# First modulation of a two-block transformer kernel: a third weight quarter split into two passes, quarters loaded in halves, two pieces given to GpSimd

## The reference, cut to what matters

```python
act_lat, act_ctx = jax.nn.silu(c), jax.nn.silu(c_ctx)          # two vectors of 1024

def ada_params(cond_act, w, b):
    mod = cond_act @ w + b                                     # w: 1024 x 3072
    return jnp.split(mod, 3, axis=-1)                          # shift, scale, gate
...
sh_l, sc_l, gt_l = ada_params(act_lat, w_ada[i], b_ada[i])
u_lat = rms_norm(h_lat, norm_g[i]) * (1.0 + sc_l[:, None, :]) + sh_l[:, None, :]
sh_c, sc_c, gt_c = ada_params(act_ctx, w_ada[i], b_ada[i])
...
p_lat = u_lat @ w_in                                           # the first big product
```

## Time and profile before

| what | value |
|---|---|
| median of 3 runs | 1294.01 us (1292.58 to 1297.1) |
| the profiled execution's own time | 1294.15 us |
| its span | 1292.4 us |
| PE busy | 1279.1 us, 99% of the span |
| DVE, ACT, POOL busy | 816.0, 656.4, 443.2 us |
| first matmul of the layer's first product | 42.85 us after the span's start |

### The profile page before, as it was taken

One profiled execution on the slowest core, in us unless ns is written; L12 is line 12 of the kernel. 1 busy time (PEld: TensorE's weight loads), 2 busy tenths in 40 slices (PEclk: granted clock), 3 DMA queues, 4 the chain that ended last, 5 costly groups with the idle time before them and its releaser, 6 DMA issues.

```text
span 1292.4 us, 17472 instructions
## 1 busy us (share of the span) xinstructions
PE 1279.1 (99%) x6553; PEld 1067.3 (83%) x6553; DVE 816.0 (63%) x1215; ACT 656.4 (51%) x1074; POOL 443.2 (34%) x203
## 2 busy tenths in 40 slices
PE   8999999999999999999999999999999999999998
PEld 4688788889988888877789889888888888888886
DVE  1795788865945457788657425406448768667676
ACT  4553777844523354766654544633355534455341
POOL 0234011137432394422234333344563322332310
PEclk9999999999999999999999999999999999999999
DMA  9972000066332153312133232233255243332301
GB/s 347 310 248 74 11 23 24 27 225 203 98 98 65 35 163 98 98 49 61 48 88 99 82 82 69 79 98 98 83 161 159 86 122 107 98 113 84 114 1 66
DMA packets 181401, 135.43 MB, mean 105 GB/s; under 512 B 10154, under 2 KB 154651, under 8 KB 181324
## 3 DMA queue, kind: packets, MB, share of 16 engines
q1 hardware_dynamic: 181122, 134.34, 34.3%
q10 hardware_dynamic: 202, 0.06, 0.0%
HBM read 129.66 MB, written 4.72 MB: 104 GB/s over the span
## 4 chain that ended last, share of the span: by engine, by line
PE 87%; DVE 4%; ACT 3%; DMA 2%; issue 2%; POOL 2%; SPq 0%; DVEq 0%; POOLq 0%; ACTq 0%
PE psum L2344 26%; PE psum L2346 26%; PE psum L2345 26%; PE psum L2556 2%; POOL w_lo L773 1%; DMA ada_w<-in_w_ada 1%; PE psum L2402 1%; PE psum L2546 1%; DVE out_rows L2277 1%; PE psum L2547 1%; PE psum L2820 1%; PE psum L2808 1%; ACT w_hi L881 1%; PE psum L2831 0%; DMA w_raw<-in_mla_w_out 0%
## 5 line engine op out<-in xcount | busy, mean ns | idle before, releaser
L773 POOL TENSOR_TENSOR w_lo<-w_raw,w_hi 128x1024 fp32r<-128x1024 f32 x148 | 381.6, 2584 | 658.3 <-ACT w_hi L881 623.2
L2344 PE MATMUL psum<-u_hi,w_hi 128*128 128x512 f32 (+1 forms) x704 | 267.1, 379 | 0.7 <-POOL w_lo L773 0.5
L2345 PE MATMUL psum<-u_lo,w_hi 128*128 128x512 f32 (+1 forms) x704 | 260.9, 371 | 0.0
L2346 PE MATMUL psum<-u_hi,w_lo 128*128 128x512 f32 (+1 forms) x704 | 260.8, 370 | 0.0
L881 ACT ACTIVATE w_hi<-w_raw 128x1024 fp32r<-128x1024 f32 x148 | 155.5, 1055 | 77.3 <-PE psum L2346 28.3
L2344 PE MATMUL psum<-y_hi,w_hi 128*128 128x512 f32 x416 | 162.2, 390 | 0.0
L2345 PE MATMUL psum<-y_lo,w_hi 128*128 128x512 f32 x416 | 161.9, 389 | 0.0
L2346 PE MATMUL psum<-y_hi,w_lo 128*128 128x512 f32 x416 | 161.9, 389 | 0.0
L2344 PEld LDWEIGHTS psum<-u_hi,w_hi 128*128 128x128 f32 x704 | 132.7, 189 | 26.7 <-issue 2.4
L2346 PEld LDWEIGHTS psum<-u_hi,w_lo 128*128 128x128 f32 x704 | 132.7, 188 | 23.3
L2345 PEld LDWEIGHTS psum<-u_lo,w_hi 128*128 128x128 f32 x704 | 132.9, 189 | 20.6 <-issue 0.2
(11 more groups left out here) (498 smaller groups left out, 2586.8 us busy)
## 6 DMA issues: line engine op xcount, KB each, us to landing
w_raw<-in_w_in SPq DMA_DIRECT2D x52, 512.0 KB, 3.8
w_raw<-in_w_up SPq DMA_DIRECT2D x32, 512.0 KB, 4.1
down_set<-in_w_down SPq DMA_DIRECT2D x32, 512.0 KB, 4.9
ada_back<-in_w_ada SPq DMA_DIRECT2D x7, 2048.0 KB, 10.8
w_raw<-in_fno_w_in SPq DMA_DIRECT2D x16, 512.0 KB, 4.0
ada_w<-in_w_ada SPq DMA_DIRECT2D x3, 2048.0 KB, 15.5
w_raw<-in_mla_w_in SPq DMA_DIRECT2D x11, 512.0 KB, 5.2
w_raw<-in_mla_w_out SPq DMA_DIRECT2D x8, 512.0 KB, 3.8
```

The lines of the kernel that those rows point to most:

```text
L773: pool.tensor_tensor(WL[:, j, :], RAW[:, j % 2, :], f(WH[:, j, :]), ALU.subtract).then_inc(lo_done, 1)
L2344: pe.matmul(out, ah, bh, start=first, stop=False, skip_group_check=more)
L2345: pe.matmul(out, ah, bl, start=False, stop=False, skip_group_check=more)
L2346: return pe.matmul(out, al, bh, start=False, stop=last, skip_group_check=more)
```

## The change

Quarter 2 is now treated as quarter 1 is: ACT makes its `QHI` (one buffer for both quarters, so quarter 1's pieces wait until quarter 2's have been used), and PE multiplies it in two passes. Quarters 2, 1 and 3 are loaded in two DMAs of 1 MB each, and quarter 3's halves are put behind weight tiles 0 and 1. Of each split quarter the first `QLOW` piece is made by POOL, the other three by DVE. On DVE the pieces of quarter 2 come ahead of `DIAG`, and the last two of quarter 1 behind `first_modulation(0)`. On ACT `split_hi` of weight tile 0 comes straight after the last `QHI` piece. Semaphore names and counts follow (not shown here). The core of the diff:

```diff
@@ sync
-            sp.dma_start(AQ[2][:], ada_weights(2)).then_inc(s_adaq[2], 16)
-            for q in (1, 3):
-                sp.dma_start(AQ[q][:], ada_weights(q)).then_inc(s_adaq[q], 16)
+            def ada_half(q, n):
+                sp.dma_start(AQ[q][:, 4 * n:4 * n + 4, :], ada_weights(q)[:, 4 * n:4 * n + 4, :]).then_inc(second_half[q] if n else s_adaq[q], 16)
+            for q in (2, 1):
+                ada_half(q, 0)
+                ada_half(q, 1)
...
-            load_tile(A0, None, 0, d["mla_w_in"][:, 0:P], KC)
-            load_tile(A0, None, 1, d["mla_w_in"][:, P:2 * P], KC)
+            for n in range(2):
+                load_tile(A0, None, n, d["mla_w_in"][:, n * P:(n + 1) * P], KC)
+                ada_half(3, n)
@@ gpsimd
+            for n, q in enumerate((2, 1)):
+                pool.wait_ge(x_copied, KC + 4 * n + 1)
+                pool.tensor_tensor(QLOW[q][:, 0:2, :], AQ[q][:, 0:2, :], f(QHI[:, 0:2, :]), ALU.subtract).then_inc(l_up, 1)
             for j in range(4):
                 split_lo(A0, None, j)
@@ scalar
+            def quarter_hi(q, n):
+                if n % 2 == 0:
+                    act.wait_ge(second_half[q] if n else s_adaq[q], 16)
+                if q == 1:
+                    act.wait_ge(diag_done, n) if n else act.wait_ge(l_up, 1)
+                act.activation(QHI[:, 2 * n:2 * n + 2, :], AQ[q][:, 2 * n:2 * n + 2, :], ACT.Copy).then_inc(x_copied, 1)
             ada_row_copy(0, 0, 1)
+            for n in range(4):
+                quarter_hi(2, n)
+            act.wait_ge(spread_mm, 2)
+            quarter_hi(1, 0)
+            quarter_hi(1, 1)
             ada_row_copy(1, 2, 2)
-            act.wait_ge(s_adaq[1], 16)
-            for n in range(4):
-                act.activation(QHI[:, 2 * n:2 * n + 2, :], AQ[1][:, 2 * n:2 * n + 2, :], ACT.Copy).then_inc(x_copied, 1)
+            quarter_hi(1, 2)
+            quarter_hi(1, 3)
+            split_hi(A0, None, 0)
...
-            ada_row_copy(2, 1, 4)
-            split_hi(A0, None, 0)
             for c in range(4):
+                if c == 2:
+                    ada_row_copy(2, 1, 4)
                 lat_hi(c)
@@ vector
             v.wait_ge(s_const, 16)
+            link(v.tensor_tensor(SEL4[:], IDENT[0:4, 0:2], IDENT[0:4, 2:4], ALU.add))
+            def quarter_lo(q, n):
+                v.wait_ge(x_copied, KC + (5 if q == 1 else 1) + n)
+                k = slice(2 * n, 2 * n + 2)
+                v.tensor_tensor(QLOW[q][:, k, :], AQ[q][:, k, :], f(QHI[:, k, :]), ALU.subtract).then_inc(diag_done, 1)
+            for n in range(1, 4):
+                quarter_lo(2, n)
             for m in range(TT):
                 v.tensor_scalar(DIAG[:, m, :], IDENT[:], RSC[:, m:m + 1], None, ALU.mult).then_inc(diag_done, 1)
-            link(v.tensor_tensor(SEL4[:], IDENT[0:4, 0:2], IDENT[0:4, 2:4], ALU.add))
             v.wait_ge(spread_mm, 1)
             v.tensor_copy(BROW[:], PB[:, 0:TOEP]).then_inc(bias_row, 1)
-            for n in range(4):
-                v.wait_ge(x_copied, KC + n + 1)
-                k = slice(2 * n, 2 * n + 2)
-                v.tensor_tensor(QLOW[:, k, :], AQ[1][:, k, :], f(QHI[:, k, :]), ALU.subtract).then_inc(diag_done, 1)
+            quarter_lo(1, 1)
...
                 first_modulation(half)
+                if half == 0:
+                    quarter_lo(1, 2)
+                    quarter_lo(1, 3)
@@ tensor
-            ada(2)
-            pe.wait_ge(diag_done, TT)
+            pe.wait_ge(cact_done, 4)
+            for k in range(KC):
+                pe.wait_ge(x_copied, KC + k // 2 + 1)
+                mm = pe.matmul(ada_row_bank(2)[0:4, :], CSPLIT[:, k, :], QHI[:, k, :], start=k == 0, stop=False)
+            mm.then_inc(spread_mm, 1)
+            for k in range(KC):
+                pe.wait_ge(diag_done, k // 2) if k >= 2 else pe.wait_ge(l_up, 1)
+                mm = pe.matmul(ada_row_bank(2)[0:2, :], CSPLIT[:, k, 0:2], QLOW[2][:, k, :], start=False, stop=k == KC - 1)
+            mm.then_inc(ada_mm, 1)
+            pe.wait_ge(diag_done, 3 + TT)
             for m in range(TT):
                 mm = pe.matmul(bank(3, P, m * P), ONES[:], DIAG[:, m, :], start=True, stop=True)
             mm.then_inc(spread_mm, 1)
             turn_row(0, 0)
             turn_row(1, 2).then_inc(ada_mm, 1)
```

More of the change, by code:

```diff
@@ L191, in build @@
         DIAG = at("rstd_diag", 160, [P, TT, P])
-        AROW = [at(f"ada_row{n}", 164 - 2 * n, [2, T]) for n in range(2)]
+        AROW = [at("ada_row0", 164, [2, T]), at("ada_row1", 162, [4, T])]
         AROW += [at("ada_row2", 166, [4, T]), at("ada_row3", 204, [2, T])]
@@ L200, in build @@
         AACC = [at("ada_sum0", 156, [P, T]), at("ada_sum1", 158, [P, T]), at("ada_sum2", 204, [P, T])]
-        QHI, QLOW = at("ada_second_hi", 120, [P, KC, T], f32r), at("ada_second_lo", 136, [P, KC, T], f32r)
+        QHI = at("ada_quarter_hi", 120, [P, KC, T], f32r)
+        QLOW = {2: at("ada_third_lo", 32, [P, KC, T], f32r), 1: at("ada_second_lo", 136, [P, KC, T], f32r)}
         CSPLIT, SEL4 = at("c_act_split", 155.875, [P, KC, 4], f32r), at("row_pairs", 154.625, [4, 2])
@@ L359, in build @@
         bias_row = sem("bias_row_done_then_down_lo_by_vector")
-        bias_out = sem("bias_stored")
+        bias_out = sem("ada_third_second_half_loaded_then_bias_stored")
         link_s = sem("vector_steps")
@@ L429, in build @@
         d_full = [[s_x[0], s_x[1], s_first, s_ctx], [s_bias, s_const, s_t5, s_dft]]
-        FULL0 = [[16, 16, 16, 16], [16, 16, 48, 80]]
+        FULL0 = [[16, 16, 16, 16], [32, 16, 48, 80]]
         d_sum, SUMS0 = cols_t, 1
@@ L505, in build @@
         ADA0 = 6
+        second_half = {2: bias_out, 1: s_bias, 3: kv_raw[0]}
+        UP0 = 2
         def ada_row_bank(q):
@@ L689, in _ @@
             sp.wait_ge(f_lo, KC)
-            sp.wait_ge(bias_out, 16)
+            sp.wait_ge(bias_out, 32)
             sp.dma_start(BIAS[:], bass.AP(toep, P - 1, [[TOEP - 1, P], [P * TOEP, MH], [1, T]])).then_inc(s_bias, 16)
@@ L921, in ada_row_copy @@
                 act.wait_ge(ada_mm, done)
-                act.activation(AROW[n][:], ada_row_bank(q)[0:4 if q == 1 else 2, :], ACT.Copy).then_inc(ada_row, 1)
-            ada_row_copy(0, 0, 1)
+                act.activation(AROW[n][:], ada_row_bank(q)[0:4 if q in QLOW else 2, :], ACT.Copy).then_inc(ada_row, 1)
+            def quarter_hi(q, n):
[4 more added lines that the diff above has]
+                act.activation(QHI[:, 2 * n:2 * n + 2, :], AQ[q][:, 2 * n:2 * n + 2, :], ACT.Copy).then_inc(x_copied, 1)
+            ada_row_copy(0, 0, 1)
+            for n in range(4):
[3 more added lines that the diff above has]
+            quarter_hi(1, 1)
             ada_row_copy(1, 2, 2)
-            act.wait_ge(s_adaq[1], 16)
-            for n in range(4):
-                act.activation(QHI[:, 2 * n:2 * n + 2, :], AQ[1][:, 2 * n:2 * n + 2, :], ACT.Copy).then_inc(x_copied, 1)
+            quarter_hi(1, 2)
+            quarter_hi(1, 3)
+            split_hi(A0, None, 0)
             def lat_hi(c):
@@ L981, in head_hi @@
             def head_hi(h):
-                act.wait_ge(kv_raw[h % 2], 16 * (h // 2 + 2) if h % 2 else 32 * (h // 2 + 1))
+                act.wait_ge(kv_raw[h % 2], 16 * (h // 2 + 2) if h % 2 else 16 + 32 * (h // 2 + 1))
                 act.wait_ge(raw_full[h % 2], raw_count(HD, None, h))
@@ L2071, in _ @@
             for h in range(GH):
[L2072 removed]
+                v.wait_ge(l_up, UP0 + h + 1)
                 v.tensor_scalar(MN[:, h, :], bank(h), COLS[:, gb + h:gb + h + 1], 0.0, ALU.add, ALU.min).then_inc(l_min, 1)
@@ L2399, in ada @@
                 for k in range(k0, k1):
-                    if q == 0 and k == 4:
-                        pe.wait_ge(s_first, 16)
+                    if k == 4:
+                        pe.wait_ge(s_first if q == 0 else second_half[q], 16)
                     mm = pe.matmul(ada_row_bank(q)[0:2, :], CACT[:, k, :], AQ[q][:, k, :], start=k == 0, stop=k == KC - 1)
@@ L2428, in _ @@
             turn_row(1, 2).then_inc(ada_mm, 1)
-            pe.wait_ge(cact_done, 4)
             for k in range(KC):
-                pe.wait_ge(x_copied, KC + k // 2 + 1)
+                pe.wait_ge(x_copied, KC + 4 + k // 2 + 1)
                 pe.matmul(ada_row_bank(1)[0:4, :], CSPLIT[:, k, :], QHI[:, k, :], start=k == 0, stop=False)
             for k in range(KC):
-                pe.wait_ge(diag_done, TT + k // 2 + 1)
-                mm = pe.matmul(ada_row_bank(1)[0:2, :], CSPLIT[:, k, 0:2], QLOW[:, k, :], start=False, stop=k == KC - 1)
+                pe.wait_ge(diag_done, 3 + TT + k // 2) if k >= 2 else pe.wait_ge(l_up, 2)
+                mm = pe.matmul(ada_row_bank(1)[0:2, :], CSPLIT[:, k, 0:2], QLOW[1][:, k, :], start=False, stop=k == KC - 1)
             mm.then_inc(ada_mm, 1)
```

10 lines of the change are left out of this document (5 added, 5 removed).

## The result

| kernel | median of its runs, us | runs | ratio to before, 95% interval |
|---|---|---|---|
| before | 1292.57 (1291.99 to 1297.10) | 14 | |
| changed | 1298.91 (1296.92 to 1300.58) | 14 | 1.0043 [1.0035, 1.0050] |

The ratio compares the means of the runs (1298.73 and 1293.13); the medians lie 6.3 us apart. The forecast was 1295.7 with a range of 1292.0 to 1298.0 and 9% for "slower": the time lies above the range. The profiled execution of the changed kernel took 1299.54 us, span 1297.8, against 1294.15 and 1292.4: 5.4 us more. Its page, busy time by engine, answers to the earlier trace rows: PE is still busy 99% of the span, and has 1.3 us more to do though its list is hardly longer.

A forecast was written before the change was run, and what follows sets the result against it. PE's list was taken to bound the kernel; with POOL and DVE excluding each other, quarter 3 would start at 37.49 instead of 35.96, so 1294.15 + 1.5 = 1295.7 us, range 1292.0 to 1298.0.

The forecast's parts named there:

- the reading: First 45 us: PE's list bounds the kernel, so the change counts by when the first big product can begin.
- the prices: First 45 us: durations of added work, such as hi pieces 0.95 apart, POOL's piece 2.34, SEL4's turn 1.05 us.
- The free sum: Start of quarter 3 without POOL and DVE waits: about 33.4 us, 2.5 us earlier, total 1291.6; chance 8%.
- the exclusion: POOL and DVE subtractions in the split quarters stop each other for a whole instruction; each new overlap is a wait.
- signs that I had named against the exclusion: DVE instructions at the overlaps lasting 1.22 and 0.16 us would make the prediction wrong by up to 4 us.
- the order at DIAG's boundary: DVE, after quarter 2's lo pieces, keeps its turn through DIAG to 28.46 us; POOL's quarter 1 piece waits.
- rival 1: POOL gets in between DVE's pieces and DIAG at 27.67; quarter 3 at 38.08, loss 2.1, 1296.3 us; chance 22%.
- the granted clock stayed 1.00: PE from 32 to 34 us before, busy 1.36 of 2 us at 2.4 GHz; so the clock was expected to hold.
- rival 4: PE's clock falls to 1.2 GHz for half of quarter 3, adding 3.5 us, to 1299.2 us; chance 5%.
- the base: Quarter 2 landing at 21.94; the profiled execution's 1294.15 us, also taken for the median of three, 1294.01.
- the halves, costed at nothing: Loads of quarters 2, 1, 3 in halves: no bytes moved, landings before they are needed, cost nothing.
- the rest of the list moves with the first product: After the first product, nothing else is late; later work shifts by the same amount.

The follow-up runs named there:

- e9_tile0_last_hi_filled: `e6_tile0_last` plus dummy PE matmuls only ahead of and within quarter 2's hi pass; 1292.86 us, ratio 0.9993.
- e5_filled_throughout: Changed kernel plus dummy PE matmuls in every gap from 20.9 us to the spread; 1295.63 us, ratio 1.0016.
- e2_pe_filled: Changed kernel plus eight dummy PE matmuls between quarter 2's lo pass and the wait for DIAG; 1298.86 us, ratio 1.0030.
- e4_loads_only: Kernel before with only the change's loads (halves, quarter 3 behind the first weight tiles), nothing split anew; 1293.02 us, ratio 0.9992.
- e7_tile0_last_filled: `e6_tile0_last` plus dummy PE matmuls in quarter 2's hi and lo passes, none ahead of DIAG; 1293.87 us, ratio 1.0004.
- e8_shift_only: Kernel before, nothing split and no load changed, plus 17 dummy PE matmuls ahead of quarter 3; 1298.26 us, ratio 1.0034.
- e10_loads_again: The kernel of `e4_loads_only` measured once more, against the kernel before; 1292.53 us, ratio 0.9987.
- e1_diag_first: Changed kernel with DIAG ahead of quarter 2's lo pieces on DVE, POOL keeping its two pieces; 1296.23 us, ratio 1.0017.
- e3_no_pool_pieces: Changed kernel with both quarters' first lo pieces on DVE in place of POOL; 1296.28 us, ratio 1.0015.
- e6_tile0_last: Changed kernel with DIAG first, all lo pieces on DVE, POOL's weight tile 0 held until DVE's last piece; 1293.56 us, ratio 0.9998.
- e11_changed_hi_filled: Changed kernel plus dummy PE matmuls only ahead of and within quarter 2's hi pass; 1301.60 us, ratio 1.0052.
- the last four kernels: The final group of four follow-up kernels, measured on one chip where the kernel before took 1294.42 us (25 runs).

## Why the prediction was wrong

**Right: the reading and the prices.** PE's list in the first 45 us set the loss, and the durations held: hi pieces 0.95 apart, POOL's piece 2.39 (2.34 taken), DVE's blocked piece 4.77 - 2 x 1.14 = 2.49 (about 2.5), SEL4's turn 1.03 at full clock (1.05 taken). The free sum, quarter 3 at 33.4, is close to what `e9_tile0_last_hi_filled` measured once every exclusion and every gap in PE's work was removed: 33.28. It is not the same order, since all low pieces are DVE's there.

**Right: the exclusion.** The Trainium skill's page "SBUF — State Buffer", section "Who interferes with whom", has it as a lock for a whole instruction; the runs agree at each overlap (2.97 for DIAG, 4.55 for two pieces, 1.38 at L1603) and where they are parted (0.87, 2.36, 0.16). DIAG and POOL exclude each other, as I assumed: its first instruction lasted until POOL was done. Two of the signs that I had named against the exclusion did come, 1.21 for DVE's first lo piece of quarter 1 and 0.16 for L1603; they don't speak against it, because each began after POOL's piece had ended (31.23 after 29.90, 34.64 at 34.64).

**Wrong: the order at DIAG's boundary.** "POOL's piece of quarter 1 is ready at 26.67, while DVE runs subtractions and then DIAG with no wait between": I let DVE keep its turn to the end of DIAG (28.46). POOL got in at the boundary, and DIAG ended at 30.57 (rival 1: 30.7). With the clock held, `e5_filled_throughout` begins quarter 3 at 37.73, between the forecast's 37.49 and rival 1's 38.08. In that run this error is worth about 0.2 us. It also opened PE's pause of 2.27, but filling that pause alone did not keep the clock up (`e2_pe_filled`).

**Wrong: the clock.** That "the granted clock stayed 1.00" in one stretch, "so I expect it to hold", was the step that failed, and the 5% for rival 4 with it. That stretch is microseconds with pauses behind a dense stretch; the change replaces that dense stretch itself, the 7 us of quarter 2, by a pass with pauses.

The fourteen profiles sort without exception, by what PE did from the end of the bias matmuls to the spread. Dense or filled up to the spread (before, `e4_loads_only`, `e5_filled_throughout`, `e7_tile0_last_filled`, `e8_shift_only`, `e9_tile0_last_hi_filled`, `e10_loads_again`): no fall before 46 us. Gaps left (the changed kernel and its repeat, `e1_diag_first`, `e2_pe_filled`, `e3_no_pool_pieces`, `e6_tile0_last`, `e11_changed_hi_filled`): a fall in every one, 3.4 to 6.9 us long in all. The mean granted clock of the executions, profiled or not, agrees: 0.993 to 0.997 in all 20 of the changed kernel, 0.999 to 1.000 in the ten of `e5_filled_throughout` and in the eleven of `e7_tile0_last_filled`. Without a profile there is an exception: one of the eleven of `e1_diag_first` shows 1.000. And a pause alone does not do it: before had one of 1.04 ahead of quarter 2 and kept 1.00. With the clock held, `e5_filled_throughout` took 1295.63, near the forecast, though on another chip and with the second fall in its profile.

Rival 4's place was off as well: it was not quarter 3 that ran slowly but the turns and the passes of quarter 1, for 2.08 us, not 3.5. The Trainium skill's page "TensorE: Matmul & The Clock Gate", section "Why this matters for your kernels", warns of idle gaps between bursts. That gaps matter the runs bear out, but the gaps in its advice are longer than any here: these were 0.2 to 2.3 us, and the measurement decides.

**Mis-sized: the base.** The prediction measured itself against quarter 2's landing at 21.94, one draw. Where it lands early, before's first product comes about 1.1 earlier, near 41.7 (an estimate: 42.85 less 1.11). That fits `e6_tile0_last` and `e7_tile0_last_filled`, which at 41.2 and 41.5 take the time of before, and it fits the halves, costed at nothing, being the one part that pays: with them PE never waited for quarter 2, and two series give 0.9992 and 0.9987, of which only the second lies clear of 1. No run parts the halves from the new place of quarter 3's load. How often before draws the late landing, two profiles can't say. Its executions of 1292.80 us or less, near the 1292.53 of `e4_loads_only`'s profile, are 10 of 14 in the result's series, but 2 of 29, 10 of 28 and 5 of 25 in the three others. The forecast took one profile (1294.15) and the median of three executions (1294.01) as its base; the 14 of the result have a median of 1292.57.

**Not foreseen: the second fall.** That "the rest of the list moves with the first product" left out 1.5 us near 148. The changed kernel has it in one profile and not in the other, and `e8_shift_only` has it unsplit, so I can't charge it to the change; what sets it is open. Before may not be free of such stretches: of its 25 executions beside the last four kernels, ten have a mean granted clock of 1.000 (1291.97 to 1295.30 us) and four have 0.997, the four slowest (1296.91 to 1297.85).

The account of the profiled execution, in us: the new order with its exclusions 1.84 (44.69 - 42.85), low clock before the first product 2.08, second fall 1.5: 5.4. The forecast had 1.5 for the first and nothing for the others. Against the earlier landing the first term would be about 3.0 and the sum 6.5 (an estimate from 41.7), which would fit the 6.3 between the medians; no profile shows it.

## What to carry to other kernels

- Before you trade one long, dense TensorE instruction stream for a shorter one fed piecewise, price the stretch at the lower clock as the likeliest case, not as a remote rival: here 6.8 us at 1.2 GHz cost 2.08 us (46.77 against 44.69), and 3.4 us cost 0.96 (41.19 against 40.23).
- Where GpSimd and VectorE both have subtractions ready, treat every boundary between two VectorE instructions as one where GpSimd may get in, and put what the path needs (here DIAG) ahead of the contended stretch and GpSimd's unhurried work behind it by a wait: with that, and all low pieces on VectorE, the first product came at 41.19, not 46.77.
- Dummy matmuls held the clock where they left PE no gap up to the spread (`e5_filled_throughout`, `e7_tile0_last_filled`, `e9_tile0_last_hi_filled`), and not where some were left (`e2_pe_filled`, `e11_changed_hi_filled`). Only those that end before the real operand is ready are free: fillers in the lo pass too cost 1.3 us (41.50 against 40.23).

## What the runs showed of the hardware that was not expected

- A fall of the granted clock with pauses of 0.2 to 0.3 us between matmul pairs and one of 1.6 ahead of them (`e6_tile0_last`: 0.50 from 24 to 26 us).

```profile
24.00:26.00 2.00, 1.96 (x5) 0.43 (x6) 2.00 (x3) 0.94 (x1) 0.00 (x0) 0.50 1.07 360
```

- The same instructions can run at the low clock in one execution and not in another: from 24 to 26 us `e2_pe_filled` was at 0.50 and the changed kernel, the same up to there, at 1.00; near 147 us the changed kernel fell to 0.50 in one profile and held 1.00 in the other, which fell near 307 instead.
- GpSimd got in between two VectorE instructions that were both ready, in every profile where it was ready at the boundary: ahead of DIAG in the changed kernel, its repeat, `e2_pe_filled`, `e5_filled_throughout` and `e11_changed_hi_filled`, and between the last two lo pieces in `e1_diag_first` and `e3_no_pool_pieces`. In the trace of before it had once waited through three. What decides was not found.
